# Paged decode attention: half of the key pages gathered by GpSimd instead of fetched by SyncE

## What is computed

```python
past_c = pool_ckv[page_table]          # (8, 16 pages, 128, 256)
past_p = pool_kpe[page_table]          # (8, 16 pages, 128, 32)
s_past = (jnp.einsum('bthr,bnsr->bhtns', q_lat, past_c)
          + jnp.einsum('bthp,bnsp->bhtns', q_pe, past_p))
...
pr = jax.nn.softmax(s, axis=-1)        # over past and new positions
out = jnp.einsum('bhtns,bnsr->bthr', pr_past, past_c) + ...
```

## Time and profile before

| | |
|---|---|
| time, median of 3 runs | 1631.87 us (1629.93 to 1635.8) |
| the profiled execution | 1622.42 us, its span 1620.6 us |
| PE busy | 1537.4 us of the span, 95% |
| POOL busy | 62.3 us, 4%, of which 61.2 us are its 64 gathers |
| key pages, SP | 128 transfers of 144 KB, 2.4 us to landing (median) |

### The profile page before, as it was taken

One profiled execution on the slowest core, in us unless ns is written; L12 is line 12 of the kernel. 1 busy time (PEld: TensorE's weight loads), 2 busy tenths in 40 slices (PEclk: granted clock), 3 DMA queues, 4 the chain that ended last, 5 costly groups with the idle time before them and its releaser, 6 DMA issues.

```text
span 1620.6 us, 18890 instructions
## 1 busy us (share of the span) xinstructions
PE 1537.4 (95%) x7224; PEld 1237.2 (76%) x7224; DVE 893.9 (55%) x1799; ACT 245.0 (15%) x495; POOL 62.3 (4%) x72
## 2 busy tenths in 40 slices
PE   4999987879999999999999899999999999999995
PEld 3887744558888888888888687888888888888884
DVE  2174273623576676776763323434776766767635
ACT  3000022411110101101122211011101001011222
POOL 0002014330000000000000000000000000000000
PEclk9999997989999999999999899999999999999997
DMA  7203479342122222222222112022222222222201
GB/s 300 96 26 108 132 247 263 106 118 78 65 91 78 78 78 79 83 99 79 92 79 107 54 53 78 27 81 79 78 78 79 90 93 78 78 78 92 78 26 56
DMA packets 39276, 152.36 MB, mean 94 GB/s; under 512 B 6609, under 2 KB 19314, under 8 KB 26386
## 3 DMA queue, kind: packets, MB, share of 16 engines
q1 hardware_dynamic: 34066, 134.37, 24.0%
q0 software_dynamic: 5120, 16.78, 3.6%
HBM read 148.11 MB, written 3.02 MB: 93 GB/s over the span
## 4 chain that ended last, share of the span: by engine, by line
PE 91%; DVE 3%; DMA 2%; POOL 1%; issue 1%; ACT 1%; SPq 1%; POOLq 0%; DVEq 0%; ACTq 0%
PE psum L435 51%; PE psum L409 34%; POOL arena L378 1%; PE psum L529 1%; DMA arena<-in_keys 1%; PE psum L394 1%; PE psum L653 1%; PE psum L634 1%; DMA arena<-in_state 1%; PE psum L564 0%; PE psum L600 0%; PE psum L514 0%; PE psum L699 0%; ACT A L715 0%; SPq L319 0%
## 5 line engine op out<-in xcount | busy, mean ns | idle before, releaser
L435 PE MATMUL psum<-arena 128*128 128x272 f32 x1536 | 362.5, 393 | 0.0
L435 PEld LDWEIGHTS psum<-arena 128*128 128x128 f32 x1536 | 292.6, 190 | 59.4
L930 DVE TENSOR_TENSOR arena<-psum,arena 128x272 f32<-128x272 f32 x448 | 197.8, 442 | 212.8 <-PE psum L435 196.2
L409 PE MATMUL psum<-A,ring 128*128 128x272 f32 x1088 | 254.0, 396 | 0.0
L409 PEld LDWEIGHTS psum<-A,ring 128*128 128x128 f32 x1088 | 208.3, 192 | 45.0 <-issue 2.5
L409 PE MATMUL psum<-B,ring 128*128 128x272 f32 x1024 | 242.3, 400 | 0.4 <-DVE B L1216 0.4
L409 PEld LDWEIGHTS psum<-B,ring 128*128 128x128 f32 x1024 | 198.1, 194 | 41.7 <-DVE B L1216 0.5
L435 PE MATMUL psum<-B,ring 128*128 128x272 f32 x512 | 127.9, 393 | 0.9 <-DVEq L896 0.9
L435 PE MATMUL psum<-A,ring 128*128 128x272 f32 x512 | 127.9, 393 | 0.9 <-DVEq L896 0.9
L435 PE MATMUL psum<-arena,ring 128*128 128x272 f32 x512 | 127.8, 393 | 0.0
L435 PEld LDWEIGHTS psum<-B,ring 128*128 128x128 f32 x512 | 97.5, 191 | 21.0 <-DVEq L896 1.3
(11 more groups left out here) (182 smaller groups left out, 1256.1 us busy)
## 6 DMA issues: line engine op xcount, KB each, us to landing
ring<-in_weights SPq DMA_DIRECT2D x99, 1024.0 KB, 4.8
arena<-in_keys SPq DMA_DIRECT2D x128, 144.0 KB, 2.4
arena<-in_attw SPq DMA_DIRECT2D x1, 3072.0 KB, 22.9
h<-in_xT SPq DMA_DIRECT2D x1, 2176.0 KB, 9.0
out_yT<-A SPq DMA_DIRECT2D x8, 272.0 KB, 2.3
arena<-in_pemb SPq DMA_DIRECT2D x2, 544.0 KB, 6.5
arena<-in_rows,vidx POOLq DMA_INDIRECT x64
arena<-in_bias SPq DMA_DIRECT2D x1, 640.0 KB, 6.5
```

The source lines that it names most:

```text
L409: last = pe.matmul(slot(t)[0:w.shape[-1], i, 0:TH], w, x[:, k, TH * i:TH * i + TH], start=k == 0, stop=k == ks - 1)
L435: end = pe.matmul(bank(g, n), lhs[:, c, :], x(c), start=c == 0, stop=c == 3)
L930: ins = dve.tensor_tensor(out, bank(g, n), more, ALU.add)
```

## The change

GpSimd gathers the key pages of sequences 2 and 3 of each group of four, by rows, with two more columns of indices per step; SyncE fetches those of sequences 0 and 1 and loads two page numbers instead of four. The score pairs wait for both. The index table holds value and key indices and becomes `ids`. GpSimd's list is reordered, so that key steps stand between value steps.

```diff
-                _, pages = nc.values_load_multi_w_load_instructions(pt[0:1, 4 * s:4 * s + 4], engines=[sp.engine],
+                _, pages = nc.values_load_multi_w_load_instructions(pt[0:1, 4 * s:4 * s + 2], engines=[sp.engine],
                                                                     min_val=0, max_val=POOL - 1)
-                for bb in range(4):
+                for bb in range(2):
                     sp.dma_start(kring[:, s % 4, bb, :, :].rearrange("p c n -> p (c n)"),
                                  a["keys"][bass.ds(pages[bb], 1), :, :].rearrange("o p n -> (o p) n"))\
                       .then_inc(k_loaded[s % 4], 16)
...
-            pool.wait_ge(vidx_loaded, 16)
-            pool.tensor_scalar(vidx[:, 0, :], vidx[:, 0, :], 64, None, ALU.mult).then_inc(vidx_step, 1)
-            pool.wait_ge(vidx_step, 1)
-            pool.tensor_tensor(vidx[:, 0, :], vidx[:, 0, :], vidx[:, 1, :], ALU.add).then_inc(vidx_step, 1)
-            pool.wait_ge(vidx_step, 2)
+            pool.wait_ge(pids_loaded, 16)
+            pool.tensor_scalar(ids[:, 0, 0:64], ids[:, 0, 0:64], 64, None, ALU.mult).then_inc(pids_step, 1)
+            pool.tensor_scalar(ids[:, 0, 64:], ids[:, 0, 64:], 96, None, ALU.mult).then_inc(pids_step, 1)
+            pool.wait_ge(pids_step, 2)
+            pool.tensor_tensor(ids[:, 0, :], ids[:, 0, :], ids[:, 1, :], ALU.add).then_inc(pids_step, 1)
+            pool.wait_ge(pids_step, 3)
             rows = a["rows"].rearrange("o (i t) r -> (o i) (t r)", t=2)
-            pool.wait_ge(psum_full, T_QL + 1)
-            for s in range(16):
-
+            key_rows = a["keys"].rearrange("o p n -> (o p) n")
+
+            def keys(s):
+                if s >= 4:
+                    pool.wait_ge(k_scored, s // 2 - 1)
+                for bb in (2, 3):
+                    col = 64 + 2 * s + bb - 2
+                    pool.indirect_dma_start(
+                        kring[:, s % 4, bb, :, :].rearrange("p c n -> p (c n)"), None, key_rows,
+                        bass.IndirectOffsetOnAxis(ap=ids[0:96, 0, col:col + 1], axis=0)).then_inc(kg_loaded[s % 4], 16)
+
+            def values(s):
                 if s >= 2:
                     pool.wait_ge(v_used, s - 1)
                 for bb in range(4):
                     pool.indirect_dma_start(
                         vring[:, s % 2, bb, :], None, rows,
-                        bass.IndirectOffsetOnAxis(ap=vidx[:, 0, 4 * s + bb:4 * s + bb + 1], axis=0))\
+                        bass.IndirectOffsetOnAxis(ap=ids[:, 0, 4 * s + bb:4 * s + bb + 1], axis=0))\
                         .then_inc(v_loaded[s % 2], 16)
+
+            for s in range(4):
+                keys(s)
+            pool.wait_ge(psum_full, T_QL + 1)
+            values(0)
+            values(1)
+            for s in range(4, 20):
+                keys(s)
+            for r in range(6):
+                values(2 + r)
+                keys(20 + 2 * r)
+                keys(21 + 2 * r)
+            for s in range(8, 16):
+                values(s)
...
-                    pe.wait_ge(k_loaded[s % 4], 64 * (s // 4 + 1))
+                    pe.wait_ge(k_loaded[s % 4], 32 * (s // 4 + 1))
+                    pe.wait_ge(kg_loaded[s % 4], 32 * (s // 4 + 1))
```

More of the change, by code:

```diff
@@ L138, in build @@
         pt = sb("pt_ids", [1, NB * NPG], mybir.dt.int32)
-        vidx = sb("vidx", [P, 2, 64], mybir.dt.int32)
+        ids = sb("ids", [P, 2, 128], mybir.dt.int32)
         psum = ctx.enter_context(nc.psum_tensor("psum", [P, 8, 512], F))
@@ L222, in build @@
         ids_loaded = sem("ids_loaded")
-        vidx_loaded = sem("vidx_loaded")
+        pids_loaded = sem("pids_loaded")
+        kg_loaded = [sem(f"kg_loaded{i}") for i in range(4)]
         k_loaded = [sem(f"k_loaded{i}") for i in range(4)]
         v_loaded = [sem(f"v_loaded{i}") for i in range(2)]
-        vidx_step = sem("vidx_step")
+        pids_step = sem("pids_step")
         consts = sem("consts")
@@ L307, in _ @@
             sp.dma_start(arena[:, 4352:10496], a["attw"]).then_inc(attw_loaded, 16)
-            sp.dma_start(vidx[:], a["vidx"]).then_inc(vidx_loaded, 16)
+            sp.dma_start(ids[:], a["pids"]).then_inc(pids_loaded, 16)
             sp.dma_start(pt[:], a["page_table"]).then_inc(ids_loaded, 16)
@@ L1376, in lay_out @@
         "page_table": ids.reshape(1, -1),
-        "vidx": np.stack([np.concatenate([np.repeat(ids.reshape(16, 2, 4)[:, j].reshape(1, -1), 64, 0) for j in range(2)], 0),
-                          np.tile(r[:, None] % 64, (1, 64)).astype(np.int32)], 1),
+        "pids": np.stack([np.concatenate([
+            np.concatenate([np.repeat(ids.reshape(16, 2, 4)[:, j].reshape(1, -1), 64, 0) for j in range(2)], 0),
+            np.repeat(ids[:, :, 2:].reshape(1, -1), P, 0) * (r[:, None] < 96)], 1),
+            np.concatenate([np.tile(r[:, None] % 64, (1, 64)), np.tile(r[:, None] % 96, (1, 64))], 1)], 1).astype(np.int32),
         "keys": np.concatenate([pool, n["cache_kpe"][0]], 2).transpose(0, 2, 1).reshape(POOL, 3, 96, PAGE)
```

## The result

The changed kernel took **1653.41 us** (median of 4 runs, 1652.06 to 1654.34) against 1630.9 us (4 runs, 1628.62 to 1635.8) for the kernel before, a ratio of **1.0133 [1.0113, 1.0154]**: 22.5 us slower, where +4.0 us was forecast; the forecast of the time itself was 1635.9 us, with a range of 1630 to 1641.5. The profiled execution took 1652.06 us.

The account below looks back on a forecast made before the run. PE's matrix work bounds the kernel, with POOL's gathers pacing the changed loop; 3.0 - 0.5 + 1.0 + 0.5 = +4.0 us takes 1622.42 to 1626.4, and the carried 9.45 us gives 1635.9 us, range 1630 to 1641.5.

Parts of the forecast that it names:

- The step that failed: Loop, 232 to 294 us: POOL never waits, so value and key gather times simply add up to pair 15's start.
- The sign that I had: Whole kernel: the runs' median lay 9.45 us above the profiled execution, and this was carried over unchanged.
- the last stretch: Values alone, 314 to 344 us: POOL already the bound, the same 24 gathers, as long as before and 4 us later.
- the loop's term: From 232.75 us to pair 15: POOL's value and key gathers set the pace, pair 15 at 293.4 us, +3.0 us.
- ACT's and DVE's catching up: Prompt's attention behind pair 15: both engines catch up during PE's waits, which may give back 0.5 us.
- the clock: Behind pair 15: short PE waits lower its clock; a third of a 2.9 us slow spell, +1.0 us.
- DVE beside the gathers: Ahead of the loop, 203.89 to 217.80 us: eight gathers beside DVE's chain slow it, +0.5 us.
- The rule weighed in the prediction: Loop: issuers share the DMA engines, so transfers would keep the pace, pair 15 near 290 us, sum near nothing.
- Rival 1: Loop: key gathers cheap, 0.71 to 0.8 us; sum between 0 and +2, 1632 to 1634 us; chance 0.15.
- Rival 2: Loop: gathers so cheap that POOL is no bound and transfer waits vanish; at 0.5 us, 1627 us; chance 0.05.
- Rival 3: Loop: key gathers dearer than 128-row ones or held up by DVE; at 1.30 us, near 1645 us; chance 0.18.
- wrong: Listed refuting signs: POOL gaps in the loop, pair 15 awaiting SP's pages, gathers outside 0.71 to 0.95 us, changes after 420 us.

Follow-up runs that it names:

- r6: The changed kernel, unaltered, run again on an occasion of prompt increments: 1626.41 us, 1.003 against the kernel before.
- r2: The kernel before, unaltered, rerun for its own trace on an occasion of late increments: 1629.27 us, 0.9995.
- e5: The changed kernel with GpSimd gathering one key page of four per step and SyncE fetching three: 1635.35 us, 1.003 against the kernel before.
- r9: The changed kernel, unaltered, run again on another occasion of late increments: 1646.44 us, 1.0096 against the kernel before.
- e4: The changed kernel with key gathers of 128 rows instead of 96, the extra rows unread: 1626.67 us, 1.0028 against the kernel before.
- e11: The kernel before with a memset pause on GpSimd after each of its last six value steps: 1637.11 us, 1.0025.
- e10: The changed kernel with a memset pause on GpSimd after every four gathers, 20 in all: 1651.43 us, 1.012 against the kernel before.
- e2: The changed kernel with GpSimd's key gathers only for steps 0 to 19, ahead of the loop: 1623.28 us, 1.0019 against the kernel before.
- r7: Rerun of the kernel with key gathers only for steps 0 to 19, prompt increments: 1621.55 us, 0.9994 against the kernel before.
- r10: Rerun of the kernel with key gathers only for steps 0 to 19, late increments: 1628.18 us, 0.9983 against the kernel before.
- e3: The changed kernel with GpSimd's key gathers only for steps 20 to 31, those of the loop: 1626.63 us, 1.0025 against the kernel before.
- r5: Rerun of the kernel with key gathers only for steps 20 to 31, late increments: 1646.74 us, 1.0113 against the kernel before.
- r4: Rerun of the changed kernel with key gathers of 128 rows, late increments: 1647.65 us, 1.0118 against the kernel before.
- r3: The changed kernel, unaltered, rerun on an occasion of late increments: 1646.74 us, 1.0103 against the kernel before.
- e6: The kernel before with SyncE fetching two of four sequences' value rows in value steps 10 to 15, late increments: 1627.32 us, 0.998.
- r8: Rerun of the kernel before with SyncE fetching half the value rows of steps 10 to 15, prompt increments: 1623.73 us, 1.0004.
- r1: The changed kernel, unaltered, first rerun, on an occasion of late increments: 1647.67 us, 1.0098 against the kernel before.

## Why the prediction failed, step by step

**The step that failed** is "what POOL waits for (value pair r, score pair 8+r) is done more than 10 us before POOL gets there, so POOL never stands still and the rounds simply add up". The work was done in time; in the runs that count its semaphore increments were not seen in time. And there was less slack than stated: even in r6 POOL needs score pair 8 only 3.3 us after its end (234.4, gather at 237.67) and value pair 1 only 6.2 us after (236.4, gather at 242.60); some 10 us are reached in the third round. In the profile after, the increment of value pair 1 came 7.9 us after its matmuls. Rounds took 11.9 us instead of 9.9, and beyond POOL's own gaps the exchange between PE, ACT and DVE in the prompt's attention was held up: the loop's last key gather began at 300.78 and pair 15 only 14.9 us later, not 3.5. The chain by line shows the difference for 230 to 300 us. First the changed kernel where increments were prompt (r6), then the profile after:

```profile
by line: POOL arena L389 19.5%; POOL arena L381 19.0%; DMA arena<-in_rows,ids 13.6%; issue 13.6%; DMA arena<-in_keys,ids 9.3%; PE psum L555 8.2%; PE psum L590 5.2%; PE psum L679 4.2%; PE psum L660 3.2%; PE psum L669 2.2%; PE psum L564 1.2%;
```

```profile
by line: issue 26.5%; PE psum L590 15.1%; PE psum L660 14.2%; PE psum L679 14.0%; PE psum L555 13.5%; another core or an unknown queue 7.3%; PE psum L669 5.9%; DVE small L1223 1.8%; DVE rbuf L1231 1.1%; DVE small L1224 0.4%; DVE B L1239 0.4
```

In r6 the loop is a chain of gathers and their landings, as forecast; in the profile after no gather is in the first eleven places.

**The sign that I had** is the 9.45 us between the profiled execution and the median of the runs shown. I carried it over as a constant. The medians say that it was the price of such an occasion for the kernel before (8 to 9 us: 1630.4 to 1631.5 against 1622.3 to 1622.6), and in the loop it grows with the gathers. The changed kernel pays 20 to 27 us (1646.44 to 1653.41 against 1626.41). Each with the kernel before of its own occasion, that is 15.6 to 22.5 us for the change instead of 4: the term was off by 12 to 19 us. A single profiled execution is a weak sign, though: that of r2 shows late increments and took 1624.25 us, 5.0 less than its own median.

The starts in PE's timelines show where the time goes (us; the loop is counted from the first value pair to pair 15):

| | loop | pair 15 to first value pair of group two | from there to the last value pair |
|---|---|---|---|
| before, prompt (profile of before) | 59.0 | 23.5 | 33.7 |
| before, late (r2) | 60.8 | 24.4 | 37.1 |
| changed, prompt (r6) | 62.8 | 23.5 | 33.8 |
| one page, late (e5) | 72.7 | 26.2 | 37.4 |
| changed, late (profile after) | 85.6 | 26.0 | 37.4 |

Only the loop sets the kernels apart. In the last stretch late increments cost either kernel much the same, 3.4 and 3.6 us. In the loop they cost the kernel before 1.8 us and the changed one 17 to 23 (80.0 in r9 to 85.6). For the kernel before the traces account for 6.1 of the 8 to 9 us; the rest isn't found in them.

**The sum came out right where increments are prompt:** +4.0 us forecast, +3.8 between the medians of r6, +4.9 by its ratio (interval 2.9 to 6.7). Its mechanism, POOL's list as the pace of the loop, was right there; that the number fits so closely is partly luck, since the loop's term was 0.7 us too small and the three terms behind it, +1.0 us together, did not occur. By its terms, from r6's profile:

- Pair 15 at 294.07, forecast 293.4. The key gather took 0.92 us, not 0.88, and a step 1.23, so 23 steps gave 1.3 us more; the last one landed in 3.0 us instead of 3.5. The price was nearly that of the value gather; the number of rows hardly enters (0.95 for 128 rows in e4).
- ACT's and DVE's catching up (-0.5) and the clock (+1.0): neither is seen. Pair 15 to first value pair took 23.5 us, as before, at a granted clock of 1.00 both times. No row stands behind the 2.9 us from which the clock's term was made. The term exists in other runs: 5.0 to 5.9 us at 0.77 in e11 and e10.
- DVE beside the gathers (+0.5): nothing. POOL's first gather of the loop began at 232.67 against 232.75.
- The last stretch: 33.8 us against 33.7. The steps ahead of the loop are free, as expected (e2, r7, r10).

**The rule weighed in the prediction.** The Trainium skill, DMA: Bandwidth & Descriptors, section Issuing engines are not separate DMA queues, says that a second issuer saves only issue time. The DMA share of the loop fell and the time rose even in r6, so it was the issue, not the transfers, that set the pace; the sum near nothing that the rule alone would have given is excluded by r6's interval.

**The rivals.** Rival 1 (cheap gathers) falls with 0.92 us. Rival 2 (faster) needed 0.54 us. Rival 3 (slower, 1645) came near the time by another mechanism: it wanted gathers of 1.30 us, and the median gather was 0.92 and 0.95. Its lower bound was also miscounted: with the other terms' +1.0 us the sum passes 0.3% (4.9 us) from a key gather of 0.92 us on, not 0.96. What I named under "wrong" came true: gaps between POOL's gathers in the loop. That no rival was built on it is the fault: a semaphore was taken to be instantaneous.

**How far the cause is shown.** Shown: the loss comes with the loop's gathers (e3 and r5 alone give it, e2, r7 and r10 don't); it depends on the occasion, not on the rows (e4 and r4) nor on the chip (r3 and r6); it comes with late and missing increments in the trace of either kernel (r2), and only where POOL gathers; in the loop it grows with the gathers of a round (the table); and pauses take it off PE's path (e10; e11 left it open for the kernel before). Not shown: what makes the increments late. Every run here was recorded, since each lists its span and clock, and the trace with late increments also lacks many records. So it may be the recording that holds the engines up, and not the gathers by themselves. The Trainium skill, NOTIFIC — the notification-queue block, section Overflow: three behaviours, one of which stalls the engine, says that the block that writes such records holds its producers back, when it is full inside, rather than lose one. No run here shows such a stall, and none was made without records; and since a record held back in this way is not lost, the missing records need another reason. If the recording is the cause, the change costs 0.3%, and the other 0.6 to 1% is the price of looking. Load on the chip from outside the program is another candidate that no run excludes; against it, the traces of both kinds agree where POOL does not gather (the first value pair begins at 230.7 to 232.3 us in the one kind and at 229.6 to 232.4 in the other, and the lag is 0.04 us up to score pair 6). Why four of the six occasions show late increments and two don't stays open, and so does why the first result (1653.41) lies some 6 us above the three repeats of its kind (1646.44 to 1647.67).

**A better version.** None is clear of both kernels: part of the values by SyncE was 0.998 [0.9964, 0.9995] on an occasion of late increments (e6) and 1.0004 [0.9993, 1.0015] on one of prompt ones (r8).

## What to carry to other kernels

Where a profiled execution and the timed runs of the same kernel differ by more than their spread, find out what the difference is before adding it to a forecast: it is a term of its own, and the change may scale it. One execution is only a hint (r2's lay 5.0 us below its own median), so compare medians. An issuer that goes through its list without slack can turn late signals into time, so work should be moved to an engine only so far that it still stands idle between its bursts. And before a large result is explained by the change, run the unchanged and the changed kernel again on another occasion: here the same pair gave +3.8 and +22.5 us.

## What was new about the hardware

- An indirect gather by GpSimd cost 0.92 us for 96 rows of 1,536 bytes, 0.95 us for 128 rows of 1,536 bytes, and 0.95 us for 128 rows of 2,048, each the median, with 0.30 us to the next. Its price hardly depends on the rows (single gathers took up to 1.45 us).
- On some occasions semaphore increments came late while POOL gathered, most often until some 2 us after the eighth gather of an unbroken stream (gaps of 1.8 to 2.3 us in POOL's timeline, 5.9 us in DVE's in the profile after; lags of up to 8.2 us against 0.02 to 0.06 on the other occasions), in the kernels before and after alike, on four chips.
- In those traces records of increments are missing, nearly all of them of page transfers and stores beside POOL's gathers: 696 recorded in r2 from 232 to 292 us against 1,279, and 1,088 against 1,080 where only SyncE fetches.
- The stretch of short tiles behind pair 15 took 23.5 us at a granted clock of 1.00 (before and r6), 26.0 at 0.93 (after), 28.2 at 0.82 (r1) and 29.3 at 0.77 (e10). In e10 and e11, the two slowest, PE had stood still for 3.35 and 3.26 us just ahead of it.
- In the traces with late increments single register instructions of SyncE between its transfers took about 0.7 us, 18 of them in the profile after and 8 in r2, none in the profile of before.
